# Two chained transformer blocks on one core: gate and up products by rows of the weights in the middle pairs of five feed-forward layers, and two smaller moves of order

## Chip, cores and metric

One core of a Trainium2 chip runs the whole program. The metric is the time of one execution in device microseconds (us). Less is better.

## What is computed

256 tokens of width 1024 pass two blocks of two layers each, in float32. Each layer has two feed-forward layers with a mixer between them, so there are eight feed-forward layers, called f = 0 to 7 here, of this form (hidden width 2816):

```python
def swiglu_2(x, w_gate, w_up, w_down):
    return (jax.nn.silu(x @ w_gate) * (x @ w_up)) @ w_down
```

Layers 0 to 3 belong to the first block, whose modulation vectors are also computed meanwhile; layers 4 to 7 belong to the second, whose mixer has three branches: a gated delta rule, a causal depthwise convolution of 31 taps, and latent attention.

```python
h = layer_norm(DEEPNORM_ALPHA * h + 0.5 * swiglu_2(h, ...), ln1_g[l], ln1_b[l])
...
o = rms_norm(o, norm_w) * jax.nn.silu(z.reshape(...))       # the delta branch: norm of o by heads
...
h = layer_norm(DEEPNORM_ALPHA * h + mix, ln2_g[l], ln2_b[l])
```

## The kernel before

**Numbers in two parts.** Every float32 operand of a large product is held as a rounded high part and a low rest (x_hi, x_lo, w_hi, w_lo and so on). A product is three matmuls: high by high, high by low, low by high (split_mm, L945 to L950).

**The stream of weights.** The weights come as chunks of 128 x 2048 numbers (1 MB) in a fixed order for the whole program. SyncE starts the loads into a ring of five places (raw). ScalarE rounds a chunk to w_hi (L1812, a ring of four), VectorE takes the rest to w_lo (L2286), which lies over raw. ScalarE can round chunk n only when TensorE has used chunk n - 4, and chunk n + 5 can be loaded when chunk n is used. In both engines' programs the conversions stand at fixed places between the other work (convert, ahead).

**A feed-forward layer.** The hidden width is cut in 11 pairs of 128 columns (i = 0 to 10). A pair takes three chunks: rows 0 to 511 and rows 512 to 1023 of 256 gate and 256 up columns (in a chunk each of 4 row blocks k has 512 columns: 256 of the gate, then 256 of up), and 256 rows of the down matrix. In gate_up (L985) the tokens are the stationary operand, 128 at a time (t = 0, 1), and the 512 columns of weights are the moving one:

```python
last = split_mm(dst, x_hi[:, k, xs], x_lo[:, k, xs], h[:, i, :], lw[:, i, :], k == 0, k == KT - 1)
```

So the result has tokens in partitions, gate in the left half of PSUM bank t, up in the right. ScalarE takes silu of the gate half into silu_g (silu, L1868 to L1875), VectorE multiplies it with 0.5 and the up half into hid (made, L2465 to L2470). The down product needs hid with its hidden index in partitions, so TensorE turns it with four 128 x 128 transposes through PSUM bank 2 (turn_hid, L1019 to L1023); from there ScalarE rounds hid_hi (L1880) and VectorE takes hid_lo (L2309). The down product of a pair is done one pair later. TensorE's order in pair i (pair, L1053 to L1070) is: wait for both halves of hid of pair i - 1, first chunk for both tiles, turn hid of i - 1, second chunk for both tiles (8 blocks of 512-column matmul triples in all), down product of i - 1. Pairs 0, 1 and 10 are written out by themselves. Pair 2 reads hid of pair 1, and pair 9 that of pair 8.

ScalarE's order in a pair (ffn, L1866): round a chunk, hid_hi, round a chunk, silu of both tiles, round a chunk. VectorE's (ffn, L2463): the low part of a chunk, hid_lo, the low part of a chunk, made of both tiles, the low part of a chunk; in layers 0 to 3 units of the modulation (ada) stand between.

**The start of a layer.** At L1072 to L1083 TensorE does chunk b for tile 0, chunk b + 1 for tile 0, turns the second half of the input (turn_x), and then takes chunk b + 2 for tile 0 into bank 4 (EARLY). That chunk's low part is written just before by VectorE, at the end of the work on the layer norm: whole at the borders of mixer and layer 5 or 7 (ahead(n0 + 43), L3143), and in two halves, told once after the second, at the border of layers 5 and 6 (first_half, second_half, L2289 to L2299).

**The delta branch.** GpSimd computes the fourth of the channel tiles of the 31-tap convolution, a multiply (L918) and an add (L922) for each tap, and between the taps the roots that heads need (x to the power -0.5, power, L740 to L745): the root of the delta heads (head_power(call_h(l, 2), 8), L911) stands before tap 27, counted from 0. VectorE gives its argument (L2601), and waits for it. TensorE then spreads it by 8 transposes of a column (row_of, L1158, called at L1669), VectorE scales and gates the heads in two pairs (delta_scaled, L3037 to L3041, and delta_gated, L3043 to L3045), ScalarE rounds each pair to y_hi (L1965), VectorE takes y_lo (y_rest, L2593), and the branch's product begins (branch, L1685).

## Time and profile before

| what | us |
|---|---|
| median of 3 runs | 2404.59 |
| lowest and highest of them | 2402.94, 2409.56 |
| the profiled execution | 2406.93 |
| its span, first to last instruction | 2405.2 |
| TensorE busy with matmuls in the span | 2332.8 |
| VectorE busy | 1621.9 |
| ScalarE busy | 1083.3 |
| GpSimd busy | 312.1 |

The span is what the profile covers; the time of the execution is 1.7 us longer. TensorE's matmuls overlap, since each one's end lies after the start of the next, so its pace is read from the starts. Times below are counted from the start of the span.

### The profile page before, as it was taken

How to read it: one execution, taken by the hardware profiler on the slowest of the kernel's cores; microseconds unless marked ns; L12 is line 12 of the kernel's file. 1: busy time of each engine (PE TensorE's matmuls, PEld its weight loads, DVE VectorE, ACT ScalarE, POOL GpSimd, SP SyncE). 2: the span in 40 equal slices, each digit the busy share in tenths (PEclk: the TensorE clock that was granted, in tenths of full speed). 3: DMA queues.
4: the chain of work that ended last, by engine and by line, in shares of the span. 5: the costliest groups of instructions: out<-in, count | busy, mean ns of one | idle time of the engine just before them, and what ended most of it. 6: DMA issues, size and time to landing. Idle time of an engine off the chain costs nothing.

```text
span 2405.2 us, 32224 instructions
## 1 busy us (share of the span) xinstructions
PE 2332.8 (97%) x13197; PEld 1997.7 (83%) x13197; DVE 1621.9 (67%) x1805; ACT 1083.3 (45%) x1258; POOL 312.1 (13%) x421
## 2 busy tenths in 40 slices
PE   5999999999999999999999999999999999999998
PEld 4787867888888888888889889888788899998887
DVE  6898567877886766554477786745654678858544
ACT  3344555435445444444455445434343465345442
POOL 3110201101103000010001810000100006500000
PEclk9999999999999999999999999999999999999999
DMA  9996328968985576555554334556456452434663
GB/s 343 328 340 238 139 88 307 313 218 285 328 305 160 175 235 211 186 183 192 195 169 133 116 95 160 186 192 223 155 184 227 145 149 89 143 132 152 207 192 123
DMA packets 336013, 477.68 MB, mean 199 GB/s; under 512 B 23067, under 2 KB 274298, under 8 KB 335866
## 3 DMA queue, kind: packets, MB, share of 16 engines
q1 hardware_dynamic: 313050, 396.33, 50.2%
q0 software_dynamic: 22816, 79.29, 9.0%
q8 instruction: 104, 1.70, 0.3%
q14 instruction: 43, 0.35, 0.1%
HBM read 474.52 MB, written 1.05 MB: 198 GB/s over the span
## 4 chain that ended last, share of the span: by engine, by line
PE 72%; DVE 7%; issue 6%; POOLq 5%; ACT 3%; DMA 2%; DVEq 2%; POOL 1%; SPq 0%; ACTq 0%
PE ps L948 22%; PE ps L950 22%; PE ps L949 22%; POOLq L919 3%; DVE w_lo L2286 2%; POOLq L923 2%; DMA raw<-in_ffn_wu_dram 2%; PE ps L1023 1%; ACT w_hi L1812 1%; DVE mix_mem L2406 1%; DVEq L2422 1%; DVE parts L2375 1%; POOL n_rstd L751 1%; DVE mix_mem L2916 1%; PE ps L977 1%
## 5 line engine op out<-in xcount | busy, mean ns | idle before, releaser
L2286 DVE TENSOR_TENSOR w_lo<-raw,w_hi 128x2048 fp32r<-128x2048 f32 (+2 forms) x374 | 822.3, 2202 | 368.4 <-ACT w_hi L1812 363.8
L1812 ACT ACTIVATE w_hi<-raw 128x2048 fp32r<-128x2048 f32 (+2 forms) x368 | 687.2, 1867 | 455.7 <-PE ps L950 185.9
L948 PE MATMUL ps<-w_hi,x_hi 128*128 128x512 f32 x1504 | 599.5, 399 | 10.6 <-DVE x_lo L2309 5.0
L950 PE MATMUL ps<-w_hi,x_lo 128*128 128x512 f32 x1504 | 588.7, 391 | 0.0
L949 PE MATMUL ps<-w_lo,x_hi 128*128 128x512 f32 x1504 | 587.8, 391 | 0.0
L948 PEld LDWEIGHTS ps<-w_hi,x_hi 128*128 128x128 f32 x1504 | 283.8, 189 | 70.4 <-issue 7.5
L950 PEld LDWEIGHTS ps<-w_hi,x_lo 128*128 128x128 f32 x1504 | 283.4, 188 | 61.0
L949 PEld LDWEIGHTS ps<-w_lo,x_hi 128*128 128x128 f32 x1504 | 284.2, 189 | 56.6 <-issue 0.5
L948 PE MATMUL ps<-x_hi,w_hi 128*128 128x256 f32 (+1 forms) x992 | 288.0, 290 | 0.5 <-ACT mix_mem L2190 0.4
L950 PE MATMUL ps<-x_hi,w_lo 128*128 128x256 f32 (+1 forms) x992 | 282.6, 285 | 0.0
L949 PE MATMUL ps<-x_lo,w_hi 128*128 128x256 f32 (+1 forms) x992 | 282.5, 285 | 0.0
L948 PE MATMUL ps<-w_hi,hid_hi 128*128 128x512 f32 x640 | 252.8, 395 | 5.5 <-DVE hid L2470 3.8
L950 PE MATMUL ps<-w_hi,hid_lo 128*128 128x512 f32 x640 | 249.9, 390 | 0.0
L949 PE MATMUL ps<-w_lo,hid_hi 128*128 128x512 f32 x640 | 249.7, 390 | 0.0
L948 PEld LDWEIGHTS ps<-x_hi,w_hi 128*128 128x128 f32 (+1 forms) x992 | 191.6, 193 | 2.6 <-issue 0.8
L949 PEld LDWEIGHTS ps<-x_lo,w_hi 128*128 128x128 f32 (+1 forms) x992 | 191.6, 193 | 0.7 <-issue 0.5
L950 PEld LDWEIGHTS ps<-x_hi,w_lo 128*128 128x128 f32 (+1 forms) x992 | 191.3, 193 | 0.0
L1880 ACT ACTIVATE hid_hi<-ps 128x512 fp32r<-128x512 f32 (+1 forms) x96 | 53.9, 561 | 262.2 <-PE ps L1023 262.2
L751 POOL TENSOR_TENSOR n_rstd<-n_moment,half_neg 128x1 f32<-128x1 f32 x24 | 22.4, 933 | 1122.2 <-DVE n_moment L2379 903.1
L1875 ACT ACTIVATE silu_g<-ps 128x256 f32<-128x256 f32 x176 | 66.5, 381 | 188.9 <-PE ps L950 188.7
L948 PEld LDWEIGHTS ps<-w_hi,hid_hi 128*128 128x128 f32 x640 | 120.3, 188 | 33.8 <-DVE hid L2470 5.5
L949 PEld LDWEIGHTS ps<-w_lo,hid_hi 128*128 128x128 f32 x640 | 120.4, 188 | 26.1 <-issue 1.4
(418 smaller groups left out, 2816.2 us busy)
## 6 DMA issues: line engine op xcount, KB each, us to landing
raw<-in_w_in_dram SPq DMA_DIRECT2D x96, 512.0 KB, 4.7
raw<-in_ffn_wg_dram SPq DMA_DIRECT2D x88, 512.0 KB, 4.4
raw<-in_ffn_wu_dram SPq DMA_DIRECT2D x88, 512.0 KB, 5.6
raw<-in_ffn_w_gate_dram SPq DMA_DIRECT2D x88, 512.0 KB, 4.0
raw<-in_ffn_w_up_dram SPq DMA_DIRECT2D x88, 512.0 KB, 5.0
raw<-in_ffn_wd_dram SPq DMA_DIRECT2D x80, 512.0 KB, 5.1
raw<-in_ffn_w_down_dram SPq DMA_DIRECT2D x80, 512.0 KB, 4.3
spare<-in_w_ada_dram POOLq DMA_DIRECT2D x40, 512.0 KB, 5.7
```

Source lines behind the costliest of these rows:

```text
L751: g.tensor_tensor(n_rstd[:, t:t + 1], n_moment[:, t:t + 1], half_neg[:, 0:1], ALU.pow)\
L919: pool.drain()
L923: pool.drain()
L948: pe.matmul(dst, wh, vh, start=start, stop=False, skip_group_check=True)
L949: pe.matmul(dst, wh, vl, start=False, stop=False, skip_group_check=True)
L950: return pe.matmul(dst, wl, vh, start=False, stop=stop_, skip_group_check=True)
L977: last = pe.transpose(ps[:, 4 + 2 * t + half, i * P:i * P + P], src[:, t, k * P:k * P + P], ident[:])
L1023: last = pe.transpose(ps[:, 2, at_:at_ + P], hid[:, at_:at_ + P], ident[:])
L1812: return f(w_hi[at.hi_slot()][:, cols], raw[at.raw_slot()][:, cols], ACT.Copy)
L1875: f(silu_g[:, t * T:t * T + T], ps[:, gu_bank(i, t), 0:T], ACT.Silu).then_inc(gate_read, 1)
L1880: f(hid_hi[:, t0:t0 + n, :, :], ps[:, 2, 2 * P * t0:2 * P * (t0 + n)] .rearrange("p (t k n) -> p t k n", t=n, k=2), ACT.Copy).then_inc(hid ...
L2286: return v.tensor_tensor(w_lo[s][:, cols], raw[s][:, cols], w_hi[at.hi_slot()][:, cols].bitcast(F32), ALU.subtract)
```

## The change

Part one: in layers 3 to 7, pairs 2 to 8 (35 pairs) compute gate and up with the weights as stationary operand, 128 columns at a time, and all 256 tokens as moving one. x_hi and x_lo lie in one tile x_both, so one matmul of 512 columns gives high weights by high and low tokens, in the left and right half of a bank; a second of 256 columns adds low weights by high tokens to the right half. Each of the four column blocks has a bank. The halves are summed afterwards: ScalarE copies the left halves to SBUF, VectorE adds the right ones, and the rest is as before. The result has the hidden index in partitions already, so nothing is turned, and hid is rounded from SBUF.

Part two: the root of the delta heads stands before tap 25, and the two pairs of heads are both scaled, then both gated. Part three: chunk b + 2 at the starts of layers 5, 6 and 7 is told by halves, and TensorE takes its first two row blocks after the first half.

```diff
@@ -78,8 +78,8 @@
 xt = sb("xt", [P, TT, D])
-x_hi = sb("x_hi", [P, KT, T], F32R)
-x_lo = sb("x_lo", [P, KT, T], F32R)
+x_both = sb("x_both", [P, 2, KT, T], F32R)
+x_hi, x_lo = x_both[:, 0, :, :], x_both[:, 1, :, :]
 y_hi = sb("y_hi", [P, KT, T], F32R)
@@ -465,6 +468,25 @@
+BY_ROWS = (3, 4, 5, 6, 7)
+def by_rows(f, i):
+    return f in BY_ROWS and 2 <= i < PAIRS - 2
+def row_pairs(f, i):
+    return sum(1 for n in range(f) for j in range(PAIRS) if by_rows(n, j)) + \
+        sum(1 for j in range(min(i, PAIRS)) if by_rows(f, j))
+def turns(f, count):
+    return f * 12 + count - row_pairs(f, count)
+def row_banks(b):
+    return ((0, 1), (3, 2))[b]
 def gu_bank(i, t):
@@ -906,7 +928,7 @@
                 head_power(call_h(l, 1), 4)
-            if sh == 27:
+            if sh == 25:
                 head_power(call_h(l, 2), 8)
@@ -977,14 +999,14 @@
-    def gate_up(s, half, t, bank=None):
+    def gate_up(s, half, t, bank=None, ks=range(4)):
         xs = slice(t * P, t * P + P)
-        for i in range(4):
+        for i in ks:
             k = 4 * half + i
@@ -1050,7 +1072,56 @@
+        def rows(s, half, bank, col):
+            h = w_hi[s[0]][:].rearrange("p (k n) -> p k n", k=4)
+            lw = w_lo[s[1]][:].rearrange("p (k n) -> p k n", k=4)
+            both = ps[:, bank, :].rearrange("p (a n) -> p a n", a=2)
+            for i in range(4):
+                k = 4 * half + i
+                pe.matmul(both, h[:, i, col:col + P], x_both[:, :, k, :], start=(k == 0), stop=False,
+                          skip_group_check=True)
+                last = pe.matmul(ps[:, bank, T:2 * T], lw[:, i, col:col + P], x_hi[:, k, :], start=False,
+                                 stop=(k == KT - 1), skip_group_check=True)
+            return last
+        def row_pair(i):
+            (g0, u0), (g1, u1) = row_banks(0), row_banks(1)
+            turned_before = not by_rows(f, i - 1)
+            s = take()
+            made(i - 1, 0)
+            if turned_before:
+                made(i - 1, 1)
+            rows(s, 0, g0, 0)
+            rows(s, 0, u0, T)
+            if turned_before:
+                turn_hid((0, 1))
+                rows(s, 0, g1, P)
+                s2 = take(1)
+                rows(s2, 1, g0, 0)
+                rows(s2, 1, u0, T).then_inc(gu_ready, 1)
+                rows(s2, 1, g1, P)
+                pe.wait_ge(hid_lo_ready, f * 12 + i)
+                used(rows(s, 0, u1, T + P))
+                used(rows(s2, 1, u1, T + P))
+            else:
+                made(i - 1, 1)
+                rows(s, 0, g1, P)
+                used(rows(s, 0, u1, T + P))
+                s = take()
+                rows(s, 1, g0, 0)
+                rows(s, 1, u0, T).then_inc(gu_ready, 1)
+                rows(s, 1, g1, P)
+                used(rows(s, 1, u1, T + P))
+            s = take()
+            pe.wait_ge(hid_lo_ready, f * 12 + i)
+            down(*rows_in(s), 0)
+            used(down(*rows_in(s), 1))
         def pair(i, with_gates=False):
+            if by_rows(f, i):
+                row_pair(i)
+                return
             s = take()
@@ -1058,7 +1129,8 @@
                 gates(0)
-            turn_hid((0, 1))
+            if not by_rows(f, i - 1):
+                turn_hid((0, 1))
             s = take()
@@ -1078,8 +1150,15 @@
         turn_x(c, 1, src)
-        s2 = take(2)
-        gate_up(s2, 0, 0, EARLY)
+        if f > 4:
+            s2 = (at.n + 2) % HI_RING, (at.n + 2) % RAW_RING
+            pe.wait_ge(lo_half, f - 4)
+            gate_up(s2, 0, 0, EARLY, (0, 1))
+            pe.wait_ge(lo_ready, at.n + 3)
+            gate_up(s2, 0, 0, EARLY, (2, 3))
+        else:
+            s2 = take(2)
+            gate_up(s2, 0, 0, EARLY)
         x_ready(c, 1, 0)
@@ -1866,8 +1945,27 @@
+        def row_copies(i, t):
+            ts = slice(t * T, t * T + T)
+            g_bank, u_bank = row_banks(t)
+            if t == 0:
+                act.wait_ge(gu_ready, f_no * PAIRS + (i + 1))
+                act.wait_ge(hid_made, f_no * (2 * PAIRS) + 2 * i)
+                act.wait_ge(hid_lo_ready, f_no * 12 + i)
+            else:
+                chunk_done(b + 3 * i)
+            f(silu_g[:, ts], ps[:, g_bank, 0:T], ACT.Copy)
+            f(hid[:, ts], ps[:, u_bank, 0:T], ACT.Copy).then_inc(row_copied, 1)
         def silu(i, t, n):
+            if by_rows(f_no, i):
+                if t == 0:
+                    row_copies(i, 0)
+                    row_copies(i, 1)
+                act.wait_ge(gate_summed, 2 * row_pairs(f_no, i) + (t + 1))
+                f(silu_g[:, t * T:t * T + T], silu_g[:, t * T:t * T + T], ACT.Silu).then_inc(gate_read, 1)
+                return
             if t == 0:
@@ -1875,7 +1973,13 @@
         def hid_rounded(count, tiles):
-            act.wait_ge(hid_turned, f_no * 12 + count)
+            if by_rows(f_no, count - 1):
+                act.wait_ge(hid_made, f_no * (2 * PAIRS) + 2 * count)
+                chunk_done(b + 3 * count - 2)
+                f(hid_hi[:].rearrange("p t k n -> p k t n"),
+                  hid[:].rearrange("p (k t n) -> p k t n", k=2, t=TT), ACT.Copy).then_inc(hid_hi_ready, 1)
+                return
+            act.wait_ge(hid_turned, turns(f_no, count))
             t0, n = tiles[0], len(tiles)
@@ -2286,10 +2390,12 @@
-    def first_half():
+    def first_half(told=False):
         if at.n < ALL_CHUNKS:
             dve.wait_ge(hi_ready, at.n + 1)
-            rest_of(slice(0, chunk_cols(at.n) // 2))
+            last = rest_of(slice(0, chunk_cols(at.n) // 2))
+            if told:
+                last.then_inc(lo_half, 1)
@@ -2463,8 +2569,32 @@
+        def row_sums(i, t):
+            ts = slice(t * T, t * T + T)
+            g_bank, u_bank = row_banks(t)
+            dve.wait_ge(row_copied, 2 * row_pairs(f_no, i) + (t + 1))
+            v.tensor_tensor(silu_g[:, ts], silu_g[:, ts], ps[:, g_bank, T:2 * T], ALU.add).then_inc(gate_summed, 1)
+            v.tensor_tensor(hid[:, ts], hid[:, ts], ps[:, u_bank, T:2 * T], ALU.add)
+        def row_made(i, t):
+            ts = slice(t * T, t * T + T)
+            dve.wait_ge(gate_read, f_no * (2 * PAIRS) + (i * 2 + (t + 1)))
+            dve.drain()
+            v.scalar_tensor_tensor(out=hid[:, ts], in0=silu_g[:, ts], scalar=0.5, in1=hid[:, ts],
+                                   op0=ALU.mult, op1=ALU.mult).then_inc(hid_made, 1)
         def made(i, t):
+            if by_rows(f_no, i):
+                if t == 0:
+                    row_sums(i, 0)
+                    row_sums(i, 1)
+                    row_made(i, 0)
+                else:
+                    row_made(i, 1)
+                return
+            if by_rows(f_no, i - 1):
+                dve.drain()
             dve.wait_ge(gate_read, f_no * (2 * PAIRS) + (i * 2 + (t + 1)))
@@ -2472,6 +2602,11 @@
             dve.wait_ge(hid_hi_ready, f_no * 12 + count)
+            if by_rows(f_no, count - 1):
+                lo_of(hid_lo[:].rearrange("p t k n -> p k t n"),
+                      hid[:].rearrange("p (k t n) -> p k t n", k=2, t=TT),
+                      hid_hi[:].rearrange("p t k n -> p k t n")).then_inc(hid_lo_ready, 1)
+                return
             t0, n = tiles[0], len(tiles)
@@ -3045,12 +3180,11 @@
         delta_scaled(0)
+        delta_scaled(1)
         dve.drain()
         delta_gated(0)
-        delta_scaled(1)
+        delta_gated(1)
         y_rest(call_y(l, 1), work, 0)
-        dve.drain()
-        delta_gated(1)
         y_rest(call_y(l, 2), work, 1)
@@ -3140,7 +3274,8 @@
         scaled_x(n, 1)
-        ahead(n0 + 43)
+        first_half(True)
+        second_half()
@@ -3167,7 +3302,7 @@
                 if (l, j) != (1, 2):
-                    first_half()
+                    first_half(told=j == 2)
                 if (l, j) == (0, 2):
```

## Rows read from the trace of the kernel before

**Rows 1.** The page of the profile: the span

```profile
span 2405.2 us, 32224 instructions
```

**Rows 2.** Timeline of TensorE, a middle pair of layer 3: start us, us, engine, line, operation

```profile
904.14 0.60 PE L1023 MATMUL ps<-ident,hid 128*128 128x128 f32 x4
904.49 0.48 PE L948 MATMUL ps<-w_hi,x_hi 128*128 128x512 f32 x1
...
915.51 0.39 PE L948 MATMUL ps<-w_hi,x_hi 128*128 128x512 f32 x1
...
920.95 0.60 PE L1023 MATMUL ps<-ident,hid 128*128 128x128 f32 x4
```

**Rows 3.** Timeline of TensorE, a mixer product with 256 moving columns (48 matmuls between)

```profile
1400.36 0.28 PE L948 MATMUL ps<-x_hi,w_hi 128*128 128x256 f32 x1
...
1406.00 0.28 PE L950 MATMUL ps<-x_hi,w_lo 128*128 128x256 f32 x1
```

**Rows 4.** Timeline of TensorE, where 512 moving columns are followed by 256

```profile
261.93 0.39 PE L950 MATMUL ps<-w_hi,x_lo 128*128 128x512 f32 x1
262.16 0.28 PE L948 MATMUL ps<-x_hi,w_hi 128*128 128x256 f32 x1
262.27 0.28 PE L949 MATMUL ps<-x_lo,w_hi 128*128 128x256 f32 x1
```

**Rows 5.** Timeline of ScalarE, layer 3, the rounding of a chunk once one was used

```profile
915.77 1.92 ACT L1812 ACTIVATE w_hi<-raw 128x2048 fp32r<-128x2048 f32 x1 [2.70 <-PE ps L950]
```

**Rows 6.** Groups by line and shape, ScalarE and VectorE: xcount | busy us, mean ns

```profile
L1875 ACT ACTIVATE silu_g<-ps 128x256 f32<-128x256 f32 x176 | 66.5, 381 | 188.9 <-PE ps L950 188.7
...
L2286 DVE TENSOR_TENSOR w_lo<-raw,w_hi 128x2048 fp32r<-128x2048 f32 x342 | 784.0, 2295 | 361.7 <-ACT w_hi L1812 360.8 <-issue 0.3
L2470 DVE SCALAR_TENSOR_TENSOR hid<-silu_g,ps 128x256 f32<-128x256 f32 x176 | 72.7, 416 | 42.9 <-ACT silu_g L1875 42.7
...
L3039 DVE SCALAR_TENSOR_TENSOR work<-out_sb,cols,ps 128x512 f32<-128x512 f32 x4 | 3.0, 743 | 0.3 <-PE ps L1158 0.2
```

**Rows 7.** Timeline of TensorE, its idle time in the delta branch, both layers

```profile
1381.63 1.97 PE L1158 MATMUL ps<-ident,rstd 128*128 128x128 f32 x8 [2.83 <-POOL rstd L745]
...
1389.47 0.39 PE L948 MATMUL ps<-y_hi,w_hi 128*128 128x256 f32 x1 [1.42 <-DVE y_lo L2309]
...
2067.43 1.85 PE L1158 MATMUL ps<-ident,rstd 128*128 128x128 f32 x8 [2.08 <-POOL rstd L745]
...
2074.52 0.39 PE L948 MATMUL ps<-y_hi,w_hi 128*128 128x256 f32 x1 [1.03 <-DVE y_lo L2309]
```

**Rows 8.** Timeline of GpSimd: the tap two sooner, the root, and its last tap

```profile
1373.96 2.15 POOL L922 TENSOR_TENSOR diag<-diag,silu_g 128x232 f32<-128x232 f32 x1
...
1379.90 1.67 POOL L745 TENSOR_TENSOR rstd<-moment,half_neg 128x8 f32<-128x8 f32 x1
...
2065.70 1.67 POOL L745 TENSOR_TENSOR rstd<-moment,half_neg 128x8 f32<-128x8 f32 x1
...
2077.46 2.03 POOL L922 TENSOR_TENSOR diag<-diag,silu_g 128x226 f32<-128x226 f32 x1
```

**Rows 9.** Timeline of VectorE: the root's argument, and its last taps of layer 1

```profile
1375.87 0.17 DVE L2601 TENSOR_SCALAR moment<-ps 128x8 f32<-128x8 f32 x1 [0.30 <-PE ps L1152]
...
2062.42 0.17 DVE L2601 TENSOR_SCALAR moment<-ps 128x8 f32<-128x8 f32 x1 [0.21 <-PE ps L1152]
...
2092.41 13.45 DVE L2900 SCALAR_TENSOR_TENSOR diag<-probs,cols,diag 128x231 f32<-128x231 f32 x29
```

**Rows 10.** Timeline of TensorE and VectorE at the starts of layers 5, 6 and 7

```profile
1528.25 0.50 PE L948 MATMUL ps<-w_hi,x_hi 128*128 128x512 f32 x1 [1.54 <-DVE w_lo L2286]
...
1715.66 2.35 DVE L2286 TENSOR_TENSOR w_lo<-raw,w_hi 128x1024 fp32r<-128x1024 f32 x2
...
1718.07 0.50 PE L948 MATMUL ps<-w_hi,x_hi 128*128 128x512 f32 x1 [1.12 <-DVE w_lo L2286]
...
2216.76 0.50 PE L948 MATMUL ps<-w_hi,x_hi 128*128 128x512 f32 x1 [1.55 <-DVE w_lo L2286]
```

More of the change, by code:

```diff
@@ L301, in block_kernel @@
         hid_turned = sem("hid_turned")
+        gate_summed = sem("gate_summed")
+        row_copied = sem("row_copied")
+        lo_half = sem("lo_half")
         hid_hi_ready = sem("hid_hi_ready")
```

## The prediction

> **What bounds the kernel now.** I read the page first, then TensorE's groups and its timeline, then the other engines at the places that the change touches. The span is 2405.2 us [rows 1], and the profiled execution took 2406.93 us, 2.3 us above the median of the three runs. TensorE is busy for 97% of it, so nearly every microsecond has to come from TensorE's own stream or from the few places where it stands idle.
>
> A middle pair of a feed-forward layer has no idle time at all. From its turn of hid to the next pair's turn 16.81 us pass [rows 2]: 0.35 us for four transposes, 11.02 us for 48 matmuls of 512 columns, and 5.44 us for 24 more. So 512 columns take 5.44 / 24 = 0.227 us, and the 48 matmuls after the transposes take 0.14 us more than 48 x 0.227 = 10.88 us; most of that is the first of them. A turn of hid therefore costs TensorE 0.35 + 0.14 = 0.49 us. Elsewhere TensorE waits for named things: the root of the delta heads, 2.83 and 2.08 us; the second pair of delta heads, 1.42 and 1.03 us [rows 7]; and the low part of a chunk at the starts of layers 5, 6 and 7, 1.54, 1.12 and 1.55 us [rows 10].
>
> **Part one, the row pairs (35 of them).** Removed: one turn of hid for each row pair (pair 2 still turns the hid of pair 1, pair 9 no longer turns that of pair 8), so 7 turns in each of 5 layers. Gate and up were 48 matmuls of 512 columns, 10.88 us. They become 32 of 512 and 32 of 256: the same 24,576 columns, in 16 more matmuls. The question is what a 256-column matmul costs beside a 512-column one. No row alternates them. One bound: in a run of 256-column matmuls alone, 48 of them take 1406.12 - 1400.36, 0.120 us each [rows 3], and 32 x (0.227 + 0.120) = 11.10 us, which is 0.22 more than before. The other: where a 512-column matmul comes just before a 256-column one, both together take 262.27 - 261.93 = 0.34 us [rows 4], and 32 x 0.34 = 10.88 us, nothing more than before. The second is nearest to what the change does, because each 256-column matmul there follows a 512-column one; in the run of 256 alone the time of each may be that of the weight load before it, which a 512-column neighbour gives room. I take 0.34. Then a pair saves 0.49 us, and 35 pairs save 17.2 us; by the other bound 0.27 us and 9.5 us. I don't put a larger gain in the range, since the columns are the same.
>
> What the other engines get. ScalarE gains four copies of 256 columns, about 0.38 us each by the silu of that shape, 1.5 us in a pair; VectorE gains four sums, about 0.42 us each by the product of that shape [rows 6], 1.7 us, and a drain. Before, VectorE had 3 x 2.30 + 2 x 0.42 + a low part of hid of some 0.7, about 8.4 us of 16.8, so 10.1 now, and ScalarE is below that. Neither becomes the bound; only the order counts. In a usual row pair, counted from its start: first chunk used at 5.5, second at 10.9, down product until 16.3. ScalarE begins about 0.26 us after a use (915.77 against the end of the pair before at 915.51) [rows 2, 5]. It copies the last two blocks from 11.2 to 11.9; the second half of the sums ends at 12.7; silu has run beside it; the product of tile 0 is there at about 13.2 and that of tile 1 at 13.6. TensorE wants them at 16.3, so 3 us are left. Behind the waiting copies on ScalarE stands the rounding of the chunk for the next down product, which now begins at 12.8 in place of 11.5, and VectorE's low part of it ends at 17; it is wanted at 27. The low part of hid is ready at 5.1 and is wanted at 10.9. The chunk loads start when chunks are used, at the old places in these pairs.
>
> The tight place is pair 2. It holds both chunks until late, because bank 2 still has the turned hid: the first chunk is used at 10.0 us of the pair in place of 5.4. ScalarE's rounding of the next chunk stands ahead of its copies and runs from 10.3 to 12.2, VectorE's low part from there to 14.5, then four sums until 15.9, and the product at 16.4. TensorE wants it at 11.4 + 5.4 = 16.8. That is 0.4 us of cover, an estimate from the durations above. I cost it at nothing; if it is 0.5 us late, five layers cost 2.5 us. The load behind that chunk starts 4.6 us later and still has a whole pair.
>
> **Part two, the delta heads.** The argument of the root is there at 1376.04 in the first layer and at 2062.59 in the second [rows 9], but GpSimd takes the root at 1379.90 and 2065.70 [rows 8]. Put two taps sooner, in the first layer it starts when the add of the tap before it ends, 1373.96 + 2.15 = 1376.11, some 3.6 us sooner; in the second GpSimd is there first and now waits until 2062.6, so 3 us sooner. Both exceed or match TensorE's idle time, 2.83 and 2.08 us [rows 7], and this idle time goes whole: 4.9 us. TensorE's own column transposes are next, not a wait. What the wait on GpSimd holds up is its six last taps, over 2 us in the second layer; they ended at 2079.5 [rows 8] while VectorE's last taps, which the same reader waits for too, ended at 2105.9 [rows 9]. So that costs nothing while VectorE is the later by 26 us.
>
> Scaling both pairs before gating moves the second pair sooner and the first later by at most one scaling, 0.74 us [rows 6], less the drain that it now fills. The waits for the second pair are 1.42 and 1.03 us [rows 7], 2.45 together. The bounds: all of it, or 2.45 - 2 x 0.74 = 0.97. I take 1.8, since the first pair was ready just when TensorE reached it, and the scaling covers a drain. Sum of part two: 6.7 us.
>
> **Part three, the halves.** A half of the low part takes 2.35 / 2 = 1.18 us [rows 10], a whole one 2.30 [rows 6]. At layers 5 and 7 TensorE starts 2.30 - 1.18 = 1.1 us sooner; at layer 6 the halves are there already and the wait of 1.12 goes. The second half is told 1.18 us after the first, and two row blocks keep TensorE for 6 x 0.227 = 1.36 us, so it isn't waited for. Two halves are 0.06 us longer than one whole; the low part of the input behind them is wanted only after all 12 matmuls, 2.7 us. Sum: 3.3 us.
>
> **The sum.** 17.2 + 6.7 + 3.3 = 27.2 us off 2406.9 gives 2379.7. Off the median it would be 2377.4.
>
> A rule of the Trainium skill speaks against part one. The page "TensorE: Matmul & The Clock Gate", section "Back-to-back issue gap", gives a sustained spacing of about 81 ns for a matmul of 128 columns and 131 ns for one of 512 in a stream of loads and matmuls. Drawn as a line between the two, two matmuls of 256 would cost some 64 ns more than one of 512, an estimate from that page, and the 16 extra ones of a pair 1.0 us. The trace doesn't agree with the sizes: 0.227 us for 512 columns and 0.120 for 256.
>
> **Rivals.**
> Rival A, 256 columns cost 0.120 us here too: TensorE's time in a pair falls by 0.27 us only, so 9.5 + 6.7 + 3.3 = 19.5 us, 2387.4. For it: 48 rows in a run with the same pace [rows 3], the weights stationary as in the change. Against: the sequence of [rows 4]. Chance 0.30.
> Rival B, pairs wait for hid: the copies, sums and conversions reach TensorE too late at pair 3 of each layer, or a little in every pair. At pair 3 alone up to 0.5 us x 5; with some of A, 2390. Against: the 3 us of cover in all pairs but one. Chance 0.12.
> Rival C, slower: a fixed price on each extra weight load and matmul that a stream of one width does not show. Its place is the alternation in rows(), 560 extra matmuls. It has to eat 0.49 us a pair and the 10 us of the other parts, so it decides from (17.2 + 10.0) / 560 = 49 ns for each extra matmul. A price of that kind is in the trace: the 0.14 us that the matmuls after the transposes take in excess [rows 2], where TensorE changes from one kind of matmul to another. Half of it, 0.07 us, at each of the 560 gives 2406.9 + 39.2 - 27.2 = 2418.9. Against: the rows of two widths show 0 to 13 ns (0.120 less half of 0.227 is 0.0065 for each 256, 0.013 for two) [rows 3, 4]. Chance 0.05. By the line drawn from the Trainium skill's figures, 64 ns, it would be 2415.5.
> Rival D, the change doesn't do what it says: the root is waited for by nobody once it is sooner, because something else holds the heads, or the layer starts wait for the next chunk; parts two and three give nothing, 2406.9 - 17.2 = 2389.7. Against: VectorE idles for the same root and TensorE has no other open wait there. Chance 0.08.
> My forecast as summed: 0.45.
>
> The predicted time is the forecast's, 2380. The range reaches down to the median with the whole of the second pair's wait gone and a little more, 2373, and up past A, B and D to 2393. About 0.3% (7 us) is what a measurement of this kernel can tell from no change. All cases but C, and a poor mix of A, B and D, are over that: faster 0.88, same 0.07, slower 0.05.
>
> **What would show it.** In a row pair: starts 0.34 us apart for a 512 and a 256 together (0.35 for A), the pair's period 16.3 us (16.5 for A, over 17 for C), no transposes of hid in 35 pairs. At pair 3 no idle time of TensorE before its first matmul (0.1 to 0.5 for B). No idle time before the column transposes of the delta root, and under 0.4 us before each pair of delta heads; at the layer starts 0.0 to 0.5 in place of 1.1 to 1.6. The forecast is wrong if the period of a row pair is above 16.5 us, or if TensorE idles on hid, on the banks' copies, or on a chunk's low part inside the layers.

## The result and the profile after

The changed kernel takes 2393.51 us (median of 6 runs, 2392.03 to 2397.41) against 2405.15 us of the kernel before (6 runs, 2402.94 to 2414.01): a ratio of 0.9948, 95% interval 0.9937 to 0.9959. It is 12 us faster where 27 were forecast, and half a microsecond outside the stated range.

The page of the changed kernel: its span, and the busy time of the engines.

```profile
span 2390.3 us, 33494 instructions
PE 2325.7 (97%) x13617; PEld 2005.7 (84%) x13617; DVE 1673.3 (70%) x1947; ACT 1129.3 (47%) x1398; POOL 319.3 (13%) x421
```

The span is 14.9 us shorter, of which 2.9 us lie ahead of the first rounding of hid in layer 3, where neither order nor work was changed; what follows ("from layer 3 on" below) accounts for the other 12.0. TensorE has 420 more matmuls: 35 x 16 added, 35 x 4 taken away. VectorE and ScalarE are busy for 51 and 46 us more.

TensorE's timeline in a middle row pair of layer 4, from its first matmul over the down product to the next pair:

```profile
1118.38 0.39 PE L1082 MATMUL ps<-x_both,w_hi 128*128 128x512 f32 x1
1118.61 0.28 PE L1084 MATMUL ps<-x_both,w_lo 128*128 128x256 f32 x1
1118.72 0.40 PE L1082 MATMUL ps<-x_both,w_hi 128*128 128x512 f32 x1
1118.96 0.28 PE L1084 MATMUL ps<-x_both,w_lo 128*128 128x256 f32 x1
1119.08 0.40 PE L1082 MATMUL ps<-x_both,w_hi 128*128 128x512 f32 x1
...
1129.67 0.40 PE L970 MATMUL ps<-w_hi,hid_hi 128*128 128x512 f32 x1
...
1135.18 0.39 PE L1082 MATMUL ps<-x_both,w_hi 128*128 128x512 f32 x1
```

No transposes are left and there is no idle time, but the period is 1135.18 - 1118.38 = 16.80 us (16.79 unrounded), against 16.81 before [rows 2]. The 64 matmuls of gate and up take 11.29 us, 0.353 for a wide one (512 moving columns) and a narrow one (256), and the down product after them 5.50 in place of 5.44. The first wide one and its narrow one take 0.34 us together, as in the row that the prediction chose [rows 4]; all later couples take 0.35 to 0.36. What the turn of hid gave, 0.49 us, is gone again.

TensorE at the delta heads of both layers, and at the starts of layers 5 and 7:

```profile
1375.38 0.71 PE L1237 MATMUL ps<-ident,rstd 128*128 128x128 f32 x5
...
1380.53 0.36 PE L970 MATMUL ps<-y_hi,w_hi 128*128 128x256 f32 x1 [1.53 <-DVE y_lo L2415]
...
1520.46 0.50 PE L970 MATMUL ps<-w_hi,x_both 128*128 128x512 f32 x1 [0.48 <-DVE w_lo L2390]
...
2061.40 0.36 PE L970 MATMUL ps<-y_hi,w_hi 128*128 128x256 f32 x1 [1.37 <-DVE y_lo L2415]
...
2201.95 0.50 PE L970 MATMUL ps<-w_hi,x_both 128*128 128x512 f32 x1 [0.48 <-DVE w_lo L2390]
```

The waits for the root of 2.83 and 2.08 us [rows 7] are gone. The wait for the second pair of heads is gone too, but one of 1.53 and 1.37 us for the first pair has come. At the layer starts 0.48 us is left of 1.54 and 1.55 [rows 10], and nothing of layer 6's 1.12.

Something stands in the windows view that the prediction leaves out: the granted clock. The kernel before, in all stretches behind layer 4 in which it was low, the end apart (window, us, busy time of PE, PEld, DVE, ACT, POOL with counts, then PEclk, DMA share, GB/s):

```profile
1361.00:1364.40 3.40, 2.94 (x15) 2.65 (x14) 3.25 (x8) 0.00 (x0) 2.96 (x5) 0.50 0.47 122
1381.60:1385.00 3.40, 3.37 (x12) 3.08 (x13) 3.12 (x5) 0.00 (x0) 2.94 (x4) 0.51 0.53 183
2047.20:2050.60 3.40, 3.40 (x18) 3.40 (x18) 3.25 (x9) 0.00 (x0) 2.98 (x3) 0.51 0.10 13
2067.70:2071.10 3.40, 3.40 (x13) 3.02 (x12) 3.25 (x6) 0.23 (x1) 2.94 (x4) 0.51 0.69 242
2118.90:2125.60 6.70, 6.70 (x32) 6.70 (x33) 3.00 (x6) 0.00 (x0) 2.70 (x1) 0.50 0.34 104
```

The changed kernel, the same:

```profile
1357.70:1361.10 3.40, 3.03 (x15) 2.74 (x15) 3.25 (x8) 0.00 (x0) 2.96 (x5) 0.50 0.47 116
1426.10:1429.40 3.30, 3.30 (x17) 3.30 (x18) 2.51 (x5) 0.00 (x0) 1.78 (x1) 0.50 0.46 159
2108.70:2112.00 3.30, 3.30 (x17) 3.30 (x17) 1.81 (x2) 0.00 (x0) 2.23 (x1) 0.50 0.03 5
```

TensorE runs at the lower of its two levels (granted clock 0.5, 1.2 GHz) in these windows for 20.3 us before and for 10.0 us after. Two of the five stretches before begin within 0.2 us of the end of TensorE's wait for the root, and they are gone. The other three, and all three after, have no idle time ahead of them: TensorE was busy there, and among its matmuls of the 3.5 us before each are 17 to 30 of a single moving column. The changed kernel, just before its stretch at 1426:

```profile
1425.34 0.36 PE L1797 MATMUL ps<-ones,work 128*128 128x1 f32 x2
```

At half the clock a TensorE without idle time loses half of such a stretch, so 10.3 us less of them are worth some 5 us, an estimate. At the heads it can be read from the starts alone: the 8 column transposes and the 12 matmuls behind them took 1387.10 - 0.19 - 1381.63 = 5.28 us of work before in the first layer, and 1380.53 - 1.53 - 1375.38 = 3.62 after. The line of the kernel before that ends the first of them:

```profile
1387.10 0.36 PE L948 MATMUL ps<-y_hi,w_hi 128*128 128x256 f32 x1 [0.19 <-DVE y_lo L2309]
```

Not every low stretch costs its half. The stretches near 1357 and 2040 (later in n1) lie just ahead of a wait of TensorE for a copy of VectorE (mix_mem). Over all traces of the study, in both layers, this wait is 0 to 0.53 us where the clock was low there and 1.24 to 1.48 us where it was not, so most of the 1.7 us is taken out of the wait.

The account from layer 3 on: the idle times of TensorE over 0.35 us add up to 18.0 us before and 11.4 after, 6.6 less; the clock gives 5. Together 11.6 to 11.8, where the spans show 12.0; what is left for the row pairs is a few tenths. It holds for another trace of the changed kernel too (after_again below): from layer 3 on that one takes 1540.2 us and not 1537.1, with 1.4 us more of idle time and 3.4 us more of low clock. So two traces of one kernel can differ by 3 us here.

### The profile page after: what moved, and what is told of

Its sections match the earlier page's. It is cut to its first block, busy times and chain, and to the rows that moved or that the text cites. A ratio compares the mean times of both kernels' runs of the same rounds, so it can differ in the third digit from the quotient of the medians.

```text
span 2390.3 us, 33494 instructions
## 1 busy us (share of the span) xinstructions
PE 2325.7 (97%) x13617; PEld 2005.7 (84%) x13617; DVE 1673.3 (70%) x1947; ACT 1129.3 (47%) x1398; POOL 319.3 (13%) x421
## 4 chain that ended last, share of the span: by engine, by line
PE 81%; DVE 6%; DMA 4%; ACT 3%; issue 3%; DVEq 2%; POOL 1%; SPq 0%; POOLq 0%; ACTq 0%
PE ps L970 19%; PE ps L972 19%; PE ps L971 19%; PE ps L1082 11%; PE ps L1084 6%; DMA raw<-in_ffn_wu_dram 2%; DVE w_lo L2390 2%; ACT w_hi L1891 1%; DVE mix_mem L2512 1%; DVEq L2528 1%; PE ps L1659 1%; PE ps L1045 1%; DMA raw<-in_ffn_w_up_dram 1%; DVE parts L2481 1%; POOL n_rstd L773 1%
## 5 line engine op out<-in xcount | busy, mean ns | idle before, releaser
L2390 DVE TENSOR_TENSOR w_lo<-raw,w_hi 128x2048 fp32r<-128x2048 f32 (+1 forms) x376 | 822.9, 2192 | 375.4 <-ACT w_hi L1891 370.8
L1082 PE MATMUL ps<-x_both,w_hi 128*128 128x512 f32 x1120 | 397.3, 399 | 0.0
L970 PE MATMUL ps<-w_hi,x_both 128*128 128x512 f32 x944 | 377.2, 400 | 8.0 <-DVE x_both L2415 7.0
L972 PE MATMUL ps<-w_hi,x_both 128*128 128x512 f32 x944 | 370.0, 392 | 0.0
L971 PE MATMUL ps<-w_lo,x_both 128*128 128x512 f32 x944 | 369.3, 391 | 0.0
L1084 PE MATMUL ps<-x_both,w_lo 128*128 128x256 f32 x1120 | 314.5, 281 | 0.0
L970 PE MATMUL ps<-x_both,w_hi 128*128 128x256 f32 (+1 forms) x992 | 287.6, 290 | 0.5 <-ACT mix_mem L2294 0.4
L972 PE MATMUL ps<-x_both,w_lo 128*128 128x256 f32 (+1 forms) x992 | 282.2, 285 | 0.0
L971 PE MATMUL ps<-x_both,w_hi 128*128 128x256 f32 (+1 forms) x992 | 282.2, 284 | 0.0
L970 PEld LDWEIGHTS ps<-w_hi,x_both 128*128 128x128 f32 x944 | 178.4, 189 | 46.8 <-issue 8.5
L1084 PEld LDWEIGHTS ps<-x_both,w_lo 128*128 128x128 f32 x1120 | 211.5, 189 | 1.4
L972 PEld LDWEIGHTS ps<-w_hi,x_both 128*128 128x128 f32 x944 | 178.2, 189 | 38.4
L970 PEld LDWEIGHTS ps<-x_both,w_hi 128*128 128x128 f32 (+1 forms) x992 | 191.1, 193 | 2.6 <-issue 0.8
L971 PEld LDWEIGHTS ps<-x_both,w_hi 128*128 128x128 f32 (+1 forms) x992 | 191.3, 193 | 0.7 <-issue 0.5
```

The lines of the kernel that those rows point to most:

```text
L970: pe.matmul(dst, wh, vh, start=start, stop=False, skip_group_check=True)
L971: pe.matmul(dst, wh, vl, start=False, stop=False, skip_group_check=True)
L972: return pe.matmul(dst, wl, vh, start=False, stop=stop_, skip_group_check=True)
L1082: pe.matmul(both, h[:, i, col:col + P], x_both[:, :, k, :], start=(k == 0), stop=False, skip_group_check=True)
L1084: last = pe.matmul(ps[:, bank, T:2 * T], lw[:, i, col:col + P], x_hi[:, k, :], start=False, stop=(k == KT - 1), skip_group_check=True)
L2390: return v.tensor_tensor(w_lo[s][:, cols], raw[s][:, cols], w_hi[at.hi_slot()][:, cols].bitcast(F32), ALU.subtract)
```

## The experiments

Each is compared with the changed kernel unless it says otherwise. Some versions ran once only. In the traces the time ahead of layer 3, where nothing differs, lies between 851.1 and 857.6 us, so a single time decides little, and there the periods and stretches of the trace are read. "The stretch 4 to 5" is the time from ScalarE's tenth rounding of hid in layer 4 (the last of full width; two halves follow) to its first in layer 5, the mixer and both borders: 349.6 us before, 345.4 after; "6 to 7" is 351.5 before, 345.6 after.

### Which part brings the gain

**p23_no_rows.** `BY_ROWS = ()`: parts two and three alone.

> The changed kernel with no layer by rows, so parts two and three alone. By my reading of the two traces nearly the whole gain comes from here: 2394, the same as the changed kernel within 1 us, with a period of 16.81 us in all middle pairs. The rival, that part one is worth several microseconds that stand against a loss elsewhere, gives 2398 or more.

2393.76 us, ratio to the kernel before 0.9928 (0.9913 to 0.9943); the middle pairs are back at 16.81 us, the stretches are 344.2 and 346.0 us. The layout test r1, run beside it with part one as well, has 2393.08 us, so within 1 us all of the gain is here.

**p1_rows_only.** The reverse:

```diff
-            if sh == 25:
+            if sh == 27:
...
-                if f > 4:
+                if f > 99:
...
-                first_half(True)
-                second_half()
+                ahead(n0 + 43)
```

with the old order of scaling and gating as well.

> Part one alone: the root before tap 27, the old order of scaling and gating, and chunk b + 2 told whole. If a row pair saves 0.02 us the time is that of the kernel before, 2404 to 2405. If part one were worth what was predicted it would be 2388.

2405.28 us (10 runs, 2401.36 to 2411.52), beside 2409.94 us of the kernel before, which is high for it. The ratio is 0.9983 (0.9971 to 0.9994), so by the times it is 0.1 to 0.3% faster. The trace shows no such gain in the row pairs: they have 11.29 and 5.50 us as in the changed kernel. From layer 3 to the end it takes 1549.3 us against 1549.1 of the kernel before, but these two traces differ in the mixers, by 4.3 us more of idle time and 6.8 us less of low clock, so the periods say more than this sum.

### Why a row pair saves nothing

**r1_one_run.** One run of 512 moving columns in place of two.

```diff
-        x_both = sb("x_both", [P, 2, KT, T], F32R)
-        x_hi, x_lo = x_both[:, 0, :, :], x_both[:, 1, :, :]
+        x_both = sb("x_both", [P, KT, 2, T], F32R)
+        x_hi, x_lo = x_both[:, :, 0, :], x_both[:, :, 1, :]
...
-                        pe.matmul(both, h[:, i, col:col + P], x_both[:, :, k, :], start=(k == 0), stop=False,
+                        pe.matmul(both, h[:, i, col:col + P], x_both[:, k, :, :], start=(k == 0), stop=False,
```

> The changed kernel with x_both laid out so that the high and the low part of the 256 tokens of one row block lie beside each other: the wide matmul reads its 512 moving columns in one run in place of two runs that lie 8 KB apart. Theory R (two runs cost the wide matmul some 13 ns): a wide and a narrow matmul start 0.34 us after the pair before in place of 0.353, the 64 of a pair take 10.9 us in place of 11.29, the period of a row pair is 16.4 us in place of 16.79, and the whole is 35 x 0.4 = 14 us faster than the changed kernel, about 2380. Theory A (the price is that of changing between 512 and 256 columns, or of the 16 extra weight loads, whatever the layout): 0.353 and 16.79 stay, time 2393.

2393.08 us, ratio to before 0.9927 (0.991 to 0.9943). The timeline of TensorE, start and end of gate and up in one pair and the start of the next:

```profile
1103.32 0.39 PE L1082 MATMUL ps<-x_both,w_hi 128*128 128x512 f32 x1
...
1114.61 0.40 PE L970 MATMUL ps<-w_hi,hid_hi 128*128 128x512 f32 x1
...
1120.11 0.39 PE L1082 MATMUL ps<-x_both,w_hi 128*128 128x512 f32 x1
```

11.29 and 16.79 us as in the changed kernel. The layout costs nothing that shows; theory R falls.

**n1_all_wide.** The narrow ones made wide.

```diff
-                        last = pe.matmul(ps[:, bank, T:2 * T], lw[:, i, col:col + P], x_hi[:, k, :], start=False,
+                        last = pe.matmul(both, lw[:, i, col:col + P], x_both[:, :, k, :], start=False,
```

> The changed kernel with the narrow matmuls of a row pair made wide: low weights by high and low tokens, 512 columns into the whole bank. It adds one product that the result doesn't need (low by low), 64 matmuls of 512 columns in all. Theory N (narrow matmuls put the wide ones beside them out of step): with none, all 64 take 0.227 us, 14.5 us, and the down product after them 5.44 us. Theory L (weights as stationary operand, or the tile x_both, cost each wide matmul 10 ns): 0.237 us, 15.2 us.

TensorE's timeline, gate and up of one pair:

```profile
1159.10 0.39 PE L1082 MATMUL ps<-x_both,w_hi 128*128 128x512 f32 x1
...
1173.61 0.39 PE L970 MATMUL ps<-w_hi,hid_hi 128*128 128x512 f32 x1
```

14.51 us for 64, 0.227 each, and the down product is back at 5.44. So neither the weights as stationary operand nor x_both slow a wide matmul. Theory L falls; what slows the wide ones is a narrow neighbour. (A narrow matmul also writes only half a bank; no run separates that from its width.) The whole takes 2511 us, for the columns that it adds.

**n2_all_narrow.** Each wide one as two of 256 columns. With a second start in the same bank the sums are no longer right (the result is off by 0.62, relative), so the version serves for the pace alone.

```diff
-                        pe.matmul(both, h[:, i, col:col + P], x_both[:, :, k, :], start=(k == 0), stop=False,
+                        pe.matmul(both[:, 0, :], h[:, i, col:col + P], x_hi[:, k, :], start=(k == 0), stop=False,
+                                  skip_group_check=True)
+                        pe.matmul(both[:, 1, :], h[:, i, col:col + P], x_lo[:, k, :], start=(k == 0), stop=False,
```

> The changed kernel with each wide matmul of a row pair made two narrow ones on the same weights: 96 matmuls of 256 columns. Theory N (a price for each matmul beside its columns, some 13 ns, so that 256 columns cost 0.120 us, and a further price only where widths are mixed): 96 x 0.120 = 11.52 us and then nothing in the down product's first matmuls but the change of width, row pair 17.0 us. Theory M (the price is only that of mixing, narrow ones cost half a wide one once they are among themselves): 10.9 us.

```profile
1153.64 0.28 PE L1082 MATMUL ps<-x_both,w_hi 128*128 128x256 f32 x1
...
1165.15 0.40 PE L970 MATMUL ps<-w_hi,hid_hi 128*128 128x512 f32 x1
```

That is again TensorE's timeline: 11.51 us for 96, 0.120 each. The down product takes 5.47 and the row pair 16.98, as theory N had it. A narrow matmul costs 0.120 us among its like, 6.6 ns more than half a wide one, and two of them 13 ns more than one of twice the columns. Theory M falls.

**r2_wide_first.** In a column block the four wide ones, then the four narrow ones.

```diff
                     for i in range(4):
                         k = 4 * half + i
                         pe.matmul(both, h[:, i, col:col + P], x_both[:, :, k, :], start=(k == 0), stop=False,
                                   skip_group_check=True)
+                    for i in range(4):
+                        k = 4 * half + i
                         last = pe.matmul(ps[:, bank, T:2 * T], lw[:, i, col:col + P], x_hi[:, k, :], start=False,
```

> The changed kernel with the order in a column block changed: first the four wide matmuls of the four row blocks, then the four narrow ones, so the widths change once in eight and no more at every matmul. Theory R (two runs): the wide ones keep their 0.237 us and the narrow ones take 0.120 as in a run of their own, 1.43 us for eight in place of 1.41, row pair 16.85 us, some 1 us slower than the changed kernel in all. Theory A (alternation costs): wide ones 0.227, narrow 0.120, 1.39 us for eight, row pair 16.6 us, 6 us faster in all.

```profile
1103.26 1.07 PE L1082 MATMUL ps<-x_both,w_hi 128*128 128x512 f32 x4
1104.16 0.64 PE L1086 MATMUL ps<-x_both,w_lo 128*128 128x256 f32 x4
...
1114.45 0.40 PE L970 MATMUL ps<-w_hi,hid_hi 128*128 128x512 f32 x1
...
1119.94 0.62 PE L1082 MATMUL ps<-x_both,w_hi 128*128 128x512 f32 x2
```

11.19 us for the 64 and a period of 16.68 (11.20 and 16.69 unrounded): half of the way that theory A allowed (16.6), and opposite in sign to theory R. The one execution took 2392.34 us; the timed runs follow below. The order counts, and changes of width are what it changes.

**n3_chunk_wide_first.** In the usual row pairs the first chunk's 16 wide ones, then its 16 narrow ones, the second chunk in two such groups of 8 and 8.

```diff
+                        for bank, col in blocks[:2]:
+                            rows(s, 1, bank, col, 0)
+                        for bank, col in blocks[:2]:
+                            last = rows(s, 1, bank, col, 1)
+                        last.then_inc(gu_ready, 1)
...
```

(`part` 0 is the wide ones alone, 1 the narrow ones; the first chunk goes the same way over all four blocks.)

> The changed kernel with fewer changes of width: in the usual row pairs (not in pair 2) the first chunk's 16 wide matmuls, then its 16 narrow ones, and the second chunk in two such groups of 8 and 8. Wide-first by fours took 11.20 us for the 64 and 5.487 for the down product. Theory N with a price for each change of width, 14 changes then and 5 now: the 64 take 11.15 us or less and the period falls by 0.05 us to 16.63. If a run of narrow ones costs its own excess whatever its length, 11.2 and more.

2383.67 us in one execution. The timeline of TensorE in the same version, taken from its timed run below (best_by_chunk):

```profile
1117.77 3.79 PE L1082 MATMUL ps<-x_both,w_hi 128*128 128x512 f32 x16
1121.39 2.08 PE L1086 MATMUL ps<-x_both,w_lo 128*128 128x256 f32 x16
1123.30 2.00 PE L1082 MATMUL ps<-x_both,w_hi 128*128 128x512 f32 x8
1125.14 1.12 PE L1086 MATMUL ps<-x_both,w_lo 128*128 128x256 f32 x8
1126.10 2.00 PE L1082 MATMUL ps<-x_both,w_hi 128*128 128x512 f32 x8
1127.94 1.11 PE L1086 MATMUL ps<-x_both,w_lo 128*128 128x256 f32 x8
1128.89 0.40 PE L970 MATMUL ps<-w_hi,hid_hi 128*128 128x512 f32 x1
```

Read from start to start: 16 wide ones behind wide ones take 3.62 us (0.226 each), 8 wide ones behind narrow ones 1.84, which is 0.03 more than 8 x 0.227; 16 narrow ones take 1.91, the 0.12 of each less 7 ns for the first. So each change from narrow to wide costs some 20 ns net. The 64 take 11.12 us and the down product 5.47, a period of 16.59. The two prices explain it: 32 narrow ones at 6.6 ns and three changes at 20 ns are 0.27 us above the 16.32 us of 72 x 0.2267 for the columns alone, and with the eight changes of r2 the same sum gives 16.69.

### The order by chunks and by fours, timed

**after_again** and **best_wide_first** (the version of r2) ran side by side.

> The changed kernel itself, in the same job as the wide-first version, as its measure: 2393 to 2394, 0.5% below the kernel before.

2392.52 us, ratio to before 0.9942 (0.9925 to 0.996).

> The changed kernel with the four wide matmuls of a column block before its four narrow ones, timed beside the changed kernel. By the period of its row pairs, 16.69 us against 16.79, it is 35 x 0.1 = 3.6 us faster than the changed kernel, 0.15%. If that is lost in the mixers' spread, the two are equal.

2388.74 us, ratio to before 0.9923 (0.991 to 0.9936): 3.8 us below the changed kernel, as the periods say, though the six runs of each overlap (2385.77 to 2391.59 against 2389.32 to 2398.79).

**best_by_chunk** (the version of n3).

> The version of n3 again, timed. The row pair's period is 16.59 us against 16.79 in the changed kernel, in 30 of the 35 row pairs, and pair 2 goes by fours; with the changed kernel at 2392.5 to 2393.5 that is 7 us less, 2386, a ratio to the kernel before near 0.991. If the one look was luck of the first block, it is 2390 or more.

2385.61 us (6 runs, 2381.64 to 2386.07), ratio to before 0.9906 (0.9888 to 0.9925). It is the fastest version of the study. From layer 3 to the end it takes 1529.6 us against 1537.1 and 1540.2 in the two traces of the changed kernel, and 5.6 us of that lie in the row pairs' stretch of the layers (729.5 us from first to tenth rounding of hid, summed over five layers, against 735.1; 737.1 before). So in long runs of one width part one gives 7.6 of the 17.2 us that it was to give.

### The delta heads and the halves

**h1_halves_only.** Part three on the kernel before.

> The kernel before with part three alone. TensorE's waits at the starts of layers 5, 6 and 7 fall from 1.54, 1.12 and 1.55 us to 0.48, 0 and 0.48, as in the changed kernel: 3.2 us in all. The rival, that the waits only move to the next chunk, shows new idle time there.

The start of layer 5 on TensorE:

```profile
1524.34 0.50 PE L970 MATMUL ps<-w_hi,x_both 128*128 128x512 f32 x1 [0.48 <-DVE w_lo L2390]
```

0.48, 0 and 0.48 us: 3.2 us, as forecast. One new idle time comes behind, 0.28 us in pair 1 of layer 6, on the low part of hid (0.26 in the changed kernel, 0.73 in p23), so the rival has a small part of it. From layer 3 to the end it takes 1545.4 us against 1549.1, but this holds 3.4 us less of low clock too and is no measure of the 3.2. The one execution took 2399.12 us, beside 2407.53 of the kernel before.

**d2_order_only.** Both pairs scaled, then both gated, the root late.

> The kernel before with both pairs of delta heads scaled, then both gated, and nothing else. The wait for the root and the low clock behind it stay. By the changed kernel's trace the second pair is there 1.5 us sooner after the column transposes and the first 0.2 to 0.3 later: 1 us less for each layer, 348.6 and 350.5. If the two kinds of delay cancel, 349.6 and 351.5.

TensorE's idle times at the heads:

```profile
1383.25 1.97 PE L1237 MATMUL ps<-ident,rstd 128*128 128x128 f32 x8 [3.04 <-POOL rstd L767]
...
2068.60 1.97 PE L1237 MATMUL ps<-ident,rstd 128*128 128x128 f32 x8 [2.12 <-POOL rstd L767]
...
2074.31 0.36 PE L970 MATMUL ps<-y_hi,w_hi 128*128 128x256 f32 x1 [0.49 <-DVE y_lo L2415]
```

The waits for the heads are 0 and 0.49 us in place of 1.61 and 1.03. The stretches are 349.0 and 350.6, 0.6 and 0.9 less, and 2407.46 us beside 2407.53 in all: a gain of the waits, nothing that a single time shows. The low clock at the root's wait is still there, for 6.8 us in place of 3.4 in the first layer, which hides most of the gain there.

**d1_root_only and d1_root_again.** The root before tap 25 and nothing else, run twice.

> The kernel before with the root of the delta heads before tap 25 and nothing else. Theory C (the idle time also costs clock: before, the granted clock is 0.5 for 3.4 us behind each wait for the root): the wait goes, 4.9 us, and with it the slow 3.4 us behind it, 1.7 us for each layer; the stretch from the last hid_hi of layer 4 to the first of layer 5 falls from 349.6 to some 345, that of layers 6 to 7 from 351.5 to some 347. Theory W (the wait alone counts): 346.8 and 349.4. The wait for the first pair of heads grows, since TensorE reaches it sooner.

> The root before tap 25 alone, once more. If the missing gain in layer 6 to 7 was the run's, the stretch from the last hid_hi of layer 6 to the first of layer 7 falls to 346 to 348 us here, as 345.3 in layer 4 to 5; if it is the change's, it stays at 350.6.

The wait for the root is gone in both, and TensorE waits for each pair of heads instead, since it reaches them sooner. The first run (2402.99 us) had 0.96 and 1.21 us in the first layer, 0.50 and 1.21 in the second, and stretches of 345.3 and 350.6. The second run (2408.03 us), at the heads of both layers:

```profile
1384.32 0.36 PE L970 MATMUL ps<-y_hi,w_hi 128*128 128x256 f32 x1 [1.15 <-DVE y_lo L2415]
1386.77 0.58 PE L970 MATMUL ps<-y_hi,w_hi 128*128 128x256 f32 x1 [1.50 <-DVE y_lo L2415]
...
2069.64 0.35 PE L970 MATMUL ps<-y_hi,w_hi 128*128 128x256 f32 x1 [0.82 <-DVE y_lo L2415]
2072.09 0.39 PE L970 MATMUL ps<-y_hi,w_hi 128*128 128x256 f32 x1 [1.50 <-DVE y_lo L2415]
```

and its windows there, each pair up to the second wait and behind it:

```profile
1383.00:1386.80 3.80, 1.15 (x8) 0.81 (x7) 2.98 (x5) 1.66 (x3) 3.17 (x5) 1.00 0.27 96
1386.80:1390.20 3.40, 3.40 (x16) 3.40 (x17) 3.40 (x2) 3.40 (x5) 3.23 (x2) 0.50 0.02 5
2069.00:2072.80 3.80, 1.66 (x12) 1.49 (x13) 3.01 (x4) 2.12 (x2) 3.17 (x5) 1.00 0.19 64
2072.80:2076.20 3.40, 3.40 (x19) 3.40 (x18) 3.40 (x2) 3.32 (x5) 3.40 (x1) 0.51 0.00 0
```

Its stretches are 348.4 and 352.3 us: the low clock has moved from the root's wait to the second wait for the heads. The first run has no low clock at the heads, but in layer 6 to 7 it has one at the start of layer 7, behind the wait of 1.54 us for a low part:

```profile
2211.50:2214.90 3.40, 3.40 (x9) 2.63 (x8) 3.37 (x4) 2.25 (x3) 0.00 (x0) 0.50 0.00 0
```

The second run has one there too, and the kernel before, with the same wait, has not. This settles the first run's stretches. In 4 to 5 the idle times over 0.35 us fall from 6.3 to 3.7 us and the low clock from 6.8 to 3.4, so the waits give 2.5 of the 4.3 us and the clock 1.7. In 6 to 7 the idle times fall by 1.4 us and the low clock stays at 13.7 us in all, so 0.9 is all that comes. Theory C is right about the price, and the expectation of 347 in the second layer was wrong both times.

So the root alone takes away its own wait, gives part of it back in the waits for the heads, and keeps the clock only in some runs. With the new order TensorE waits once and not twice, and in none of the ten traces with both is the clock low at the heads. Nor does a wait of that length always bring the low clock: of the eight waits for the root (before, p1, d2 and h1), seven have it, and the one in the second layer of p1, 2.12 us, has not. What decides in a run whether the clock falls stays open.

## Why the prediction was wrong

**Part one failed, by the size of one term.** "I take 0.34" for a wide and a narrow matmul together was the step: measured 0.353, and 0.063 us more in the down product behind. In place of 17.2 us the row pairs give 0.4 to 2.0: from the first to the tenth rounding of hid, summed over the five layers, it is 737.1 us before, 735.1 after and 736.7 with part one alone. The turn's price of 0.49 us agrees with what was measured, but the 64 matmuls and the slower down product cost 11.29 + 5.50 - 10.88 - 5.44 = 0.47 more. The prediction's own sign of being wrong, a period above 16.5 us, shows it: 16.79. The 0.47 is more than the other bound too (0.22), which rival A took, so the truth lay outside the two bounds. Only rival C, at 0.05, allowed for a larger cost, and taking two samples for the two ends was the error behind the miss. The row chosen was one change from wide to narrow, where the first narrow matmul gains 7 ns [rows 4]; the other edge, from narrow to wide, does not stand in the sum. In the trace of before it is there, in a mixer:

```profile
1497.33 0.40 PE L948 MATMUL ps<-w_hi,y_hi 128*128 128x512 f32 x1
1497.56 0.40 PE L949 MATMUL ps<-w_lo,y_hi 128*128 128x512 f32 x1
1497.80 0.39 PE L950 MATMUL ps<-w_hi,y_lo 128*128 128x512 f32 x1
1498.03 0.40 PE L948 MATMUL ps<-w_hi,y_hi 128*128 128x512 f32 x1
```

0.23 to 0.24 us each behind a run of narrow ones, where 0.227 is the pace. A smaller part of the distance is the start of the sum: it takes 27.2 us off one execution of 2406.9, and the median of the kernel before is 2405.15.

**Part two was about right, for a reason that was half missing.** Forecast 6.7 us, the two stretches less the 2.1 us of the halves in them give 8.0. The root's wait went whole (4.9, as forecast). The waits for the heads did not fall: 0.19 + 1.42 + 1.03 = 2.64 us before, 1.53 + 1.37 = 2.90 after, because TensorE now arrives sooner; the prediction had put each under 0.4 us. The 1.8 us for the order were not there as a difference of the two traces, though with the root early the order is worth 1.0 to 2.1 (one wait of 1.53 and 1.37 against two in each layer, 3.88 and 4.97 together in the two runs of d1) and seems to be what keeps the clock. The granted clock, which the prediction left out, gave what was missing, some 1.7 us at each layer's heads, and shifted by as much elsewhere in the mixers. That 8.0 came so near to 6.7 is therefore in part luck. GpSimd's later last taps cost nothing, as argued.

**Part three was right**: 3.2 us measured, 3.3 forecast, with 0.26 us of new idle time behind it.

**The rivals.** A was nearest: its cause, narrow matmuls at 0.120 us, is real, but it is less than half of the cost. B fell: no idle time at pair 3 in any layer, and none on hid inside the row pairs. C named the right place, the alternation, with too large a price: some 29 ns for each extra matmul (0.47 / 16) in place of the 49 at which it decides. The Trainium skill's page "TensorE: Matmul & The Clock Gate", section "Back-to-back issue gap", gave 64 ns by a line between its two figures; the measurement decides for 13 ns in a run of one width, and up to 29 where they alternate. D did not come.

## What to carry to other kernels

A matmul has a price beside its columns, and streams that mix widths pay again at each change from narrow to wide: order them in long runs of one width, and read both edges of a change in the trace before a fraction of a microsecond is multiplied by 35. When a cost is not in the trace, the two nearest rows are samples and not bounds. An idle time of TensorE of two or three microseconds should be priced with the granted clock behind it, which cost some 1.7 us more at each wait for the root before. The clock must be compared before two single traces are: where it was low moves from run to run, also without idle time, and a low stretch ahead of another engine's wait costs little.

## What was not expected of the hardware

- 512 moving columns (float32r) take 0.227 us, 256 take 0.120 (96 in a run: 11.51 us). Alternating they take 0.353 together, 6 ns more than the sum, with 0.06 us more in the wide ones behind. In runs of 4, 8 or 16 each change from narrow to wide costs some 20 ns; in the down product behind narrow ones it is spread over five wide matmuls (233, 236, 228, 233 and 231 ns). Why it costs that is not shown.
- Whether the moving columns lie in one run or in two 8 KB apart made no difference (11.29 us both times).
- The low clock came in stretches of 3.4 or 6.8 us, 20.3 us in all before and 10.0 after. Some stand behind idle times of TensorE; most in the mixers stand behind 17 or more matmuls with a single moving column, while TensorE was busy. They are not in the same places in every run of the same kernel.
